# A decoder step whose gated feed-forward is computed by Strassen's seven products instead of plain tiles

## What is computed

```python
D_FF = 2816
def swiglu(hn, w_gate, w_up, w_down):
    return (jax.nn.silu(hn @ w_gate) * (hn @ w_up)) @ w_down
hp = rms_norm(y_p, g_ffn_pre[l])
y_p = y_p + rms_norm(swiglu(hp, w_gate[l], w_up[l], w_down[l]), g_ffn_post[l])
```

## Time and profile before

| | us |
|---|---|
| median of 3 runs | 975.21 (974.14 to 975.98) |
| the profiled execution, its span | 972.4 |
| of it, PE busy | 931.1 |
| DVE / ACT / POOL busy | 431.7 / 361.6 / 198.5 |
| chain that ended last, share of PE | 88% |
| largest line of that chain, L1854 | 58% |

### The profile page before, as it was taken

How to read it: one execution, slowest core, us unless ns; L and a number is a source line. 1 busy time by engine, 2 the same in 40 slices (tenths; PEclk the granted TensorE clock), 3 DMA queues, 4 the chain that set the end, 5 groups by cost and what they waited for, 6 DMA issues and landing times.

```text
span 972.4 us, 17713 instructions
## 1 busy us (share of the span) xinstructions
PE 931.1 (96%) x7522; PEld 860.0 (88%) x7522; DVE 431.7 (44%) x868; ACT 361.6 (37%) x570; POOL 198.5 (20%) x66
## 2 busy tenths in 40 slices
PE   4999999889999999999989999999999999999997
PEld 4999998756799889975579899999999999999996
...
DMA packets 81247, 105.84 MB, mean 109 GB/s; under 512 B 9473, under 2 KB 64642, under 8 KB 81058
## 3 DMA queue, kind: packets, MB, share of 16 engines
...
q10 hardware_dynamic: 226, 0.05, 0.0%
...
## 4 chain that ended last, share of the span: by engine, by line
PE 88%; DVE 5%; ACT 3%; issue 2%; DMA 1%; SPq 1%; DVEq 0%; POOL 0%; ACTq 0%
PE pall L1854 58%; PE pall L1866 6%; PE pall L2208 4%; PE pall L1891 4%; PE pall L1924 2%; PE pall L2259 1%; PE pall L2278 1%; PE pall L1878 1%; PE pall L2084 1%; PE pall L1975 1%; PE pall L2076 1%; DMA sel<-in_t_sel 1%; PE pall L1958 1%; PE pall L1979 1%; PE pall L2314 1%
## 5 line engine op out<-in xcount | busy, mean ns | idle before, releaser
L630 POOL TENSOR_TENSOR w_lo<-w_raw,w_hi 128x2048 fp32r<-128x2048 f32 (+1 forms) x38 | 170.3, 4482 | 460.9 <-ACT w_hi L704 378.8
L1854 PE MATMUL pall<-x_hi,w_hi 128*128 128x272 f32 x992 | 206.4, 290 | 0.5 <-issue 0.5
L1854 PE MATMUL pall<-x_lo,w_hi 128*128 128x272 f32 x992 | 205.3, 288 | 0.0
L1854 PE MATMUL pall<-x_hi,w_lo 128*128 128x272 f32 x992 | 203.9, 287 | 0.0
L1854 PEld LDWEIGHTS pall<-x_hi,w_hi 128*128 128x128 f32 x992 | 155.2, 188 | 1.4 <-issue 0.7
L1854 PEld LDWEIGHTS pall<-x_lo,w_hi 128*128 128x128 f32 x992 | 156.2, 189 | 0.0
L1854 PEld LDWEIGHTS pall<-x_hi,w_lo 128*128 128x128 f32 x992 | 155.5, 189 | 0.0
L704 ACT ACTIVATE w_hi<-w_raw 128x2048 fp32r<-128x2048 f32 (+1 forms) x60 | 113.0, 1883 | 106.6 <-PE pall L1854 92.0
L1854 PE MATMUL pall<-g_hi,w_hi 128*128 128x272 f32 x352 | 73.1, 289 | 0.0
L1854 PE MATMUL pall<-g_lo,w_hi 128*128 128x272 f32 x352 | 72.8, 288 | 0.0
L1854 PE MATMUL pall<-g_hi,w_lo 128*128 128x272 f32 x352 | 72.7, 288 | 0.0
...
## 6 DMA issues: line engine op xcount, KB each, us to landing
w_raw<-in_w_gate SPq DMA_DIRECT2D x10, 1024.0 KB, 5.3
w_raw<-in_w_up SPq DMA_DIRECT2D x10, 1024.0 KB, 5.3
w_raw<-in_w_in SPq DMA_DIRECT2D x8, 1024.0 KB, 5.7
w_raw<-in_w_down SPq DMA_DIRECT2D x8, 1024.0 KB, 5.2
dm_kv<-in_cache_mem_v SPq DMA_DIRECT2D x5, 1024.0 KB, 14.0
w_raw<-in_w_out SPq DMA_DIRECT2D x4, 1024.0 KB, 8.0
...
```

The lines of the kernel that those rows point to most:

```text
L630: e.tensor_tensor(w_lo[:, n % 2, 0:w], w_raw[:, n % 2, 0:w], w_hi[:, n % 2, 0:w].bitcast(F32), ALU.subtract)\
L1854: ins = mm(acc(j)[:, a, :], w, x[:, k_x + k, a * HALF:(a + 1) * HALF], start=first and k == 0 and s_, stop=last and k == kts - 1 and t_)
```

## The change

Gate, up and down are computed by the seven products of Strassen's scheme (in the form with shared sums). A unit's weights are a 2 x 2 of quarters: even and odd row tiles by first and second 128 columns. The tokens' matrix is a 2 x 2 as well: even and odd row tiles by the two halves of 272. Seven products of sums of quarters take the place of eight.

- **The weights.** For each unit DVE forms four sums of quarters, 128x512 each (`weight_sums`), partly in place in `w_raw`, three in `w_sum`. ACT copies each of the seven operands to a ring of eight slots of 512 floats (`ring_hi`, in the memory of `w_hi`), POOL writes the low parts (`ring_lo`). So POOL has 7 subtractions of 128x512 for a unit where it had one of 128x2048.
- **The tokens.** Four sums of the normed input are formed once (`input_sum`), and cut into high and low parts. For down, DVE forms for each pair four sums of its product's quarters (`g_sums`, `g_last`), and ACT and DVE cut seven quarters of 272 instead of four (`g_hi`, `g_low`; `g_part`).
- **PE.** A unit of 8 row tiles is 7 products of 4 x 3 = 12 matmuls of 272 columns, 84 in all, where it had 96. The three banks `sev_banks(n)` take sums of products in turn: product 2 waits until ACT has copied product 0 out (`sev_copy`), product 4 until all three copies are out, product 6 until DVE has taken product 4 (`sev_out`). Two sets of three banks alternate; banks 6 and 7 are left for the turning of `zg`.
- **Evacuation.** ACT copies three partial sums for each unit from PSUM to the tile, DVE adds the next ones to them (`sev_evac`), and multiplies.
- **Order.** The list `sev`: pairs 1 to 3, then down's four blocks for pairs 0 to 3, pairs 4 to 7 and down's blocks, pairs 8 to 10 and down's blocks. Down's output is added up over the groups in `z_down`, which lies where `yT` was; in the second and third group DVE adds the first partial sums too (`sev_add`).
- **The residual.** `yT` is stored to DRAM (`y_keep`, 2.2 MB) after the input's sums are made, and loaded to `y_back` ahead of the end.

Some semaphores of the attention stages get other names and offsets, and `z`, `t_half`, `q_half`, `wx_hi` and `wx_lo` other places; nothing is added to or taken from those stages.

The list of units, the waits of SP ahead of a load, and the residual's store:

```diff
+    sev = []
+    for first in range(0, PAIRS, GROUP):
+        pairs = range(first, min(first + GROUP, PAIRS))
+        sev += [(what, p, 4) for p in pairs if p for what in ("gate", "up")]
+        sev += [("down", (first // GROUP, c), len(pairs)) for c in range(DOWN_C)]
...
+    SEV_BANK = (0, 2, 0, 1, 0, 2, 0)
...
+        for n, (what, at_, np_) in enumerate(sev):
+            e.wait_ge(*((S("sev_lo"), 7 * (n - 1)) if n >= 2 else (w_lo_ready, U_FFN - 1 + n)))
...
+            if n == 1:
+                e.wait_ge(S("x_sum"), 4)
+                e.dma_start(y_kept, yT[:]).then_inc(S("y_kept"), 16)
```

POOL (the low parts), then ACT (`sev_hi`, the high parts):

```diff
-        with e.Fori(0, PAIRS - 1) as i:
-            for s_ in range(1, 3):
-                split_lo(U_FFN + s_, KT, 256, i, 2)
...
+            n, i = divmod(q, 7)
+            e.wait_ge(S("sev_hi"), q + 1)
+            e.tensor_tensor(w_part(ring_lo[:, q % RING, :], n), sev_source(n, i), w_part(ring_hi[:, q % RING, :], n).bitcast(F32), ALU.subtract)\
+                .then_inc(S("sev_lo"), 1)
...
+            if q < RING:
+                e.wait_ge(acc_full, J_FFN)
+            else:
+                e.wait_ge(S("sev_p"), q - RING + 1)
...
+            e.activation(w_part(ring_hi[:, q % RING, :], n), sev_source(n, i), ACT.Copy).then_inc(S("sev_hi"), 1)
```

DVE, the sums of weights:

```diff
+        def weight_sums(n, which):
...
+            if 1 in which:
+                e.wait_ge(w_loaded[sev_slot(n)], 16 * ((U_FFN + n) // 2 + 1))
+                if n:
+                    e.wait_ge(S("sev_lo"), 7 * (n - 1) + 2)
+                add(s1, a21, a22).then_inc(S("w_sum"), 1)
+                e.wait_ge(S("w_sum"), 4 * n + 1)
+                sub(a21, a21, a11).then_inc(S("w_sum"), 1)
+            if 2 in which:
+                if n:
+                    e.wait_ge(S("sev_lo"), 7 * (n - 1) + 6)
+                sub(s2, s1, a11).then_inc(S("w_sum"), 1)
+                e.wait_ge(S("w_sum"), 4 * n + 3)
+                sub(s4, a12, s2).then_inc(S("w_sum"), 1)
```

DVE, the order of its work for a unit:

```diff
+        for n, (what, at_, np_) in enumerate(sev):
...
+            if before == "up":
+                g_low(p, 0)
+                g_low(p, 1)
+            if n:
+                weight_sums(n + 1, (1,))
+            if before == "up":
+                g_low(p, 2)
...
+            if n:
+                weight_sums(n + 1, (2,))
...
+            if before == "gate":
+                for m in range(2):
+                    e.wait_ge(S("silu"), 2 * p + m + 1)
+                    mul(gate_tile(p, m), gate_tile(p, m), rstd[:])
...
+            sev_evac(n)
```

PE, the seven products of a unit:

```diff
-                for m in range(2):
-                    j = 2 * s_ + m
-                    e.wait_ge(acc_out, i * 4 + (J_LOOP + j - 1))
-                    product(m, slot, 256, m * P, x_hi, x_lo, 0, KT).then_inc(acc_full, 1)
...
+            for i in range(7):
+                q = 7 * n + i
+                if i == 0:
+                    e.wait_ge(*((S("sev_out"), 4 * (n - 1)) if n >= 2 else (acc_out, J_FFN + 3 * (n + 1))))
+                elif i in (2, 4):
+                    e.wait_ge(S("sev_copy"), 3 * n + i - 1)
+                elif i == 6:
+                    e.wait_ge(S("sev_out"), 4 * n + 2)
+                e.wait_ge(S("sev_lo"), q + 1)
...
+                for j in range(np_):
+                    xh, xl = sev_input(n, i, j)
+                    wh, wl = (r[:, q % RING, j * P:(j + 1) * P] for r in (ring_hi, ring_lo))
+                    for w, x, s_, t_ in ((wh, xh, True, False), (wh, xl, False, False), (wl, xh, False, True)):
+                        ins = mm(out, w, x, start=i in SEV_FIRST and j == 0 and s_, stop=j == np_ - 1 and t_,
+                                 skip_group_check=i not in SEV_FIRST)
+                ins.then_inc(S("sev_p"), 1)
```

More of the change, by code:

```diff
@@ L1125, in _ @@
             gained_half(1, k)
+        for i in range(3):
+            sev_hi(0, i)
         root_half("n4", bank(7), 1)
+        sev_hi(0, 3)
+        sev_hi(0, 4)
+        x_sum_hi(0)
         rows_half(bank(7), 1)
+        sev_hi(0, 5)
+        x_sum_hi(1)
+        sev_hi(0, 6)
         for m in range(2):
[L1129 to L1133 removed]
@@ new lines, in _ @@
+        x_sum_hi(2)
+        x_sum_hi(3)
+        for n, (what, at_, np_) in enumerate(sev):
+            before, p = sev[n - 1][:2] if n else ("none", 0)
+            if before == "gate":
+                silu(p, 0)
+            elif before == "up":
+                g_hi(p, 1)
+            sev_copy(n, 0)
+            sev_hi(n + 1, 0)
+            if before == "gate":
+                silu(p, 1)
+            elif before == "up":
+                g_hi(p, 2)
+            sev_copy(n, 1)
+            sev_hi(n + 1, 1)
+            sev_copy(n, 2)
+            for i in range(2, 6):
+                sev_hi(n + 1, i)
+                if n == 0 and i < 5:
+                    g_hi(0, i - 2)
+            if what == "up":
+                g_hi(at_, 0)
+            sev_hi(n + 1, 6)
+            if what == "down" and at_[0] == LAST_DOWN:
+                y_squares(n)
@@ new lines, in _ @@
+        pair_half(5)
+        input_sum(2)
+        pair_half(6)
+        input_sum(3)
+        pair_half(7)
+        input_low(2)
+        weight_sums(1, (1, 2))
+        input_low(3)
+        first_pair()
+        for n, (what, at_, np_) in enumerate(sev):
+            before, p = sev[n - 1][:2] if n else ("none", 0)
+            adds = what == "down" and at_[0] > 0
+            if before == "up":
[5 more added lines that the diff above has]
+                g_low(p, 2)
+            if adds:
+                sev_add(n, 0)
+            if n:
+                weight_sums(n + 1, (2,))
+            if adds:
+                sev_add(n, 1)
+                sev_add(n, 2)
+            if before == "gate":
+                for m in range(2):
+                    e.wait_ge(S("silu"), 2 * p + m + 1)
+                    mul(gate_tile(p, m), gate_tile(p, m), rstd[:])
+            if n == 0:
+                for i in range(3):
+                    g_low(0, i)
+            last = what == "down" and at_[0] == LAST_DOWN
+            if last and at_[1]:
+                y_square(2 * at_[1] - 2)
+                y_square(2 * at_[1] - 1)
+                zg_out(2 * at_[1] - 2)
+                zg_out(2 * at_[1] - 1)
+            sev_evac(n)
@@ L2037, in _ @@
                 e.wait_ge(S("xs_lo"), KT)
-                transposes(bank(6), [st_nat[:, r, :] for r in range(2)]).then_inc(S("stT"), 1)
+                transposes(bank(6), [st_nat[:, r, :] for r in range(2)]).then_inc(S("par_full"), 1)
                 for r in range(2):
@@ new lines, in sev_input @@
+        def sev_input(n, i, j):
+            what, at_, _ = sev[n]
+            if what == "down":
+                p = GROUP * at_[0] + j
+                if at_[1] == 0:
+                    e.wait_ge(S("g_lo"), 3 * p + G_BATCH[i])
+                return g_part[:, p % GROUP, G_PLACE[i], :], g_part[:, p % GROUP, 7 + G_PLACE[i], :]
+            if n == 0 and j == 0 and i in (1, 2, 4, 6):
+                e.wait_ge(*{1: (S("x_sum_lo"), 1), 2: (S("x_sum_lo"), 2), 4: (S("x_sum_dve"), 1), 6: (S("x_sum_dve"), 2)}[i])
+            if i in (1, 2, 4):
+                t = (None, 0, 1, None, 2)[i]
+                return x_sum[:, t, 0, j, :], x_sum[:, t, 1, j, :]
+            k, half = {0: (0, H0), 3: (1, H0), 5: (1, H1), 6: (0, H1)}[i]
+            return x_hi[:, 2 * j + k, half], x_lo[:, 2 * j + k, half]
@@ L2414, in y_transposes @@
+        for n in range(len(sev)):
+            seven(n)
+        zg_transposes(KT - 2)
         def y_transposes(t):
```

468 lines of the change are left out of this document (311 added, 157 removed).

## The result

The changed kernel takes **1031.5 us** (median of 4 runs, 1023.6 to 1032.1), the kernel before, run beside it, 975.6 (974.1 to 978.0): a ratio of 1.056, with a 95% interval of 1.052 to 1.060. The forecast was 1020 us, slower. The profiled execution took 1032.1 us, and its span is 1030.3 us: what lies around the instructions is 1.8 us. (The 2.8 us read ahead of the forecast were the median of three runs less the span of one, by the same 1.8 us the fastest of them.)

A forecast was written before the change was run, and what follows sets the result against it. The bound was to move from PE to the SBUF path POOL and DVE share. Pairs 285, down 86 and 38, handovers 6, start 3 made 418 us for 375.4, plus 2 at the end: +45, 1020 us, range 985 to 1072.

The forecast's parts named there:

- The mechanism: In the pairs, the bound moves from PE to what POOL and DVE share: 26.6 us a pair against PE's 21.0.
- rival 1: Stage of seven products: PE stays the bound and the kernel gets faster, 942 us; chance 0.08.
- sign: Pairs' trace: long `ring_lo` and sums, PE some 75% busy, waiting for POOL's `ring_lo` and DVE's adds; ACT as releaser refutes.
- The pairs: Gate and up, ten pairs: 28.5 us each, 285 us for 240, so +45 (ends +26 and +82).
- about 8 us once: In the pairs, the ring of eight lets POOL run seven products ahead, but can't carry 5 us a pair.
- The start: Ahead of unit 0: input sums on DVE, two cuts on POOL, and the residual's store; +3 us (0 to 10).
- The handovers: Three times down begins with a pair whose low parts aren't cut: some 2 us each, 6 us (0 to 12).
- Down: Down units: first eight at 10.8 us, 86 us (84 to 106); last four at 9.5, 38 us (38 to 56).
- The end: Kernel's end: squares taken from SBUF after DVE's last add, `zg` turned in one bank pair; +2 us (0 to 4).
- no change: Whole kernel within 0.2% of the old time: would need a pair of about 24.5 us; chance 0.02.
- Rival 2: Pairs: PE falls to the lower clock as well, kernel 1050 us, or over 1100 if nearly all matmuls; chance 0.14.
- Rival 3: At the start, the parked residual holds up unit 2's weights by 11 us and delays the end: 1032; chance 0.03.

The follow-up runs named there:

- e1: Changed kernel with POOL's 224 subtractions for the weights' low parts replaced by three memsets each, which write but don't read: 951.1 us, ratio 0.976.
- e2: Changed kernel with all low parts of the seven products and the input sums' two subtractions moved from POOL to DVE: 985.5 us, ratio 1.011.
- e9: e2 with the input's last low part ahead of the second unit's sums and product 3's low parts on POOL: 1000.5 us, ratio 1.025.
- e8: Changed kernel with filler matmuls of the identity into unused bank 6 in the two places where PE rests longest: 1025.7 us, ratio 1.051.

## Why the forecast was right, and where its sum was off

**The mechanism held.** PE gave way to the read path that POOL and DVE share. e1 takes away POOL's reads alone and the kernel falls to 951 us (rival 1's forecast for a kernel bound by PE was 942); e2 and e9 show the same from the other side. `ring_lo` and the sums have the lengths that the forecast named, PSUM adds are untouched, and PE waits at product 6.

**Not every sign came as named.** The forecast had PE wait for `ring_lo` on POOL as well, and would have counted ACT among PE's releasers against itself. From 585 to 1016 us no rest of PE names POOL; about 49 us name DVE and 18 name ACT. Of ACT's 18, the 7.67 us in unit 0 stand behind DVE's sums, as the rows above show. In the pairs ACT is named for 4.0 us and DVE for 11.1, of the 15 that PE rests. The shared path works through DVE's and ACT's places in the order, and PE was busy for 84% of the pairs' time and not 75%, at a clock of 0.95.

**The pairs: right in size, counted too often.** The forecast had 28.5 us a pair, ten times, 285. The seven pairs that follow another pair in their group take 26.7 to 28.8 us, 27.7 in the mean. But the ten pairs without what unit 0 lost took 266 us. The down units let POOL and ACT run ahead (PE busy for 38.1 of 38.9 us there), so the first pair behind each group is 24.1 and 23.1 us. I had named that lead, "about 8 us once", and taken nothing off for it.

**The start: +3 forecast, +15.2 measured** (29.08 us for unit 0, 13.9 for a steady gate unit). I had counted some 5 us of DVE work and set it against DVE's idle time before 583. The four-instruction groups of 272 went by POOL's turns, 7.92 us for 1.74, and behind them stood ACT's copy for PE's product 2. In proportion this term was the most wrong: five times the forecast.

**The handovers: 2 us each forecast, 6.9, 9.1 and 7.2 measured** (17.35 and 19.61 less 10.5, 16.72 less 9.5). The chain that I named is the one in the trace, but priced without POOL's turns: in e1, where POOL reads nothing, the three cost 1.5, 2.9 and 1.7 us (12.01, 13.35 and 11.22 less the same), 6.1 in all for the 6 of the forecast. The turns make a rest of 4.57, and the lower clock behind it adds some 2 us more, 3.4 at the third (e8).

**Down**: the first eight units without the handovers 85.5 us for 86; the last four 41.1 for 38. In e1 these four take 39.5, counted in the same way, so 1.5 of the 3 us go with POOL's reads; the rest is a PE time that I had put too low or waits for DVE's output work, which no run separates. **The end**: +0.5 for +2.

The stage, forecast 285 + 3 + 86 + 38 + 6 = 418, measured 266.2 + 15.2 + 85.5 + 41.1 + 23.2 = 431.2. Errors of +12 (start), +17 (handovers) and +3 (last four) against one of -19 (pairs): that the total came within 12 us of the measured time is in part luck. Two slips of the working change nothing by themselves. 418 us for 375.4 and 2 at the end are +44.6, a span of 1017.0; and by the same sum no change would need a pair of 24.0 us, not 24.5.

**Rival 2** (the lower clock) happened as a mechanism and not at its price: PE's timeline has matmuls 0.227 us apart behind a rest, for 0.125, and the mean clock in the pairs is 0.95, but e8, which restores it for some 37 of 65 us, wins about 5 us of 58. What the lower clock costs in the first units stays open. **Rival 3**: the residual's store is issued 0.38 us ahead of unit 2's load, as SP's timeline shows:

```profile
593.43 0.34 SPq L682 DMA_DIRECT2D y_keep<-yT  x1
593.81 0.44 SPq L679 DMA_DIRECT2D w_raw<-in_w_gate  x1
```

The store lands after 7.7 us. Unit 2 starts at 625.8 us, 32 us later, and none of PE's rests names a load. No kernel was run without the parking; the trace gives it no room.

**What stays open.** How much of unit 0's remaining 8 to 9 us (e1) is ACT's order alone: its copy could stand ahead of the cuts of the third and fourth input sums, which was not tried.
